# The experts' down product with the matmuls placed in column tiles of the array

## The reference, cut to what matters

```python
def expert_choice_ffn(x, w_router, w_gate, w_up, w_down):
    B, T, _ = x.shape
    cap = CAP_FACTOR * T // N_EXPERTS
    aff = jax.nn.softmax((x @ w_router).astype(jnp.float32), -1)
    gsel, idx = lax.top_k(jnp.swapaxes(aff, 1, 2), cap)
    bidx = jnp.arange(B)[:, None, None]
    xs = x[bidx, idx]
    hdn = jax.nn.silu(jnp.einsum('becd,edf->becf', xs, w_gate)) * jnp.einsum('becd,edf->becf', xs, w_up)
    out = jnp.einsum('becf,efd->becd', hdn, w_down) * gsel[..., None].astype(x.dtype)
    return jnp.zeros_like(x).at[bidx, idx].add(out)
```

## Time and profile before

| what | value |
|---|---|
| median of 3 runs | 3254.94 us (3253.11, 3254.94, 3256.28) |
| span of the profiled execution | 3254.3 us |
| PE busy | 3039.7 us, 93% |
| PE weight loads busy | 2229.6 us, 69% |
| DVE, ACT, POOL busy | 963.2, 577.3, 96.0 us |
| bytes over HBM | 517.89 MB read, 25.70 MB written |

### The profile page before, as it was taken

How to read it: one execution, slowest core, us unless ns; L and a number is a source line. 1 busy time by engine, 2 the same in 40 slices (tenths; PEclk the granted TensorE clock), 3 DMA queues, 4 the chain that set the end, 5 groups by cost and what they waited for, 6 DMA issues and landing times.

```text
span 3254.3 us, 43264 instructions
## 1 busy us (share of the span) xinstructions
PE 3039.7 (93%) x18405; PEld 2229.6 (69%) x18405; DVE 963.2 (30%) x2408; ACT 577.3 (18%) x1297; POOL 96.0 (3%) x145
## 2 busy tenths in 40 slices
PE   6999999797999999997999989999986999999994
PEld 1465479745887777771456459999944888777773
DVE  1100136643001000102177536666645010001002
ACT  3100111240000000003167212222242000000002
POOL 0000000000000000000000000000000000000000
PEclk9899998897999999998999999999997999999997
DMA  8411100217999999957411100000016899999992
GB/s 281 154 52 52 45 1 1 65 62 270 312 311 303 303 309 308 306 183 271 155 52 52 39 0 1 1 2 1 1 65 224 279 314 304 307 305 307 306 310 87
DMA packets 276365, 545.50 MB, mean 168 GB/s; under 512 B 15233, under 2 KB 23817, under 8 KB 276233
## 3 DMA queue, kind: packets, MB, share of 16 engines
q1 hardware_dynamic: 175049, 328.64, 29.4%
q10 hardware_dynamic: 93600, 188.75, 16.6%
q0 software_dynamic: 7584, 26.22, 3.2%
HBM read 517.89 MB, written 25.70 MB: 167 GB/s over the span
## 4 chain that ended last, share of the span: by engine, by line
PE 88%; DVE 6%; ACT 3%; DMA 2%; issue 1%; SPq 0%; DVEq 0%; POOL 0%; ACTq 0%
PE ps L1204 28%; PE ps L1215 14%; PE ps L803 8%; PE ps L813 6%; PE ps L760 5%; PE ps L1139 3%; PE ps L1101 3%; PE ps L804 2%; PE ps L1083 2%; PE ps L880 1%; PE ps L1115 1%; PE ps L791 1%; PE ps L950 1%; PE ps L966 1%; ACT L424 1%; ACT L423 1%
## 5 line engine op out<-in xcount | busy, mean ns | idle before, releaser
L1204 PEld LDWEIGHTS ps<-wk,slots 128*128 128x128 f32 x6144 | 691.1, 192 | 16.5 <-issue 16.0
L1204 PE MATMUL ps<-wk,slots 128*128 128x80 f32 x6144 | 689.9, 275 | 0.0
L1215 PE MATMUL ps<-qkv,og 128*80 128x512 f32 x1024 | 446.7, 594 | 2.4 <-DVE og L1748 1.3
L1215 PEld LDWEIGHTS ps<-qkv,og 128*80 128x80 f32 x1024 | 151.0, 150 | 275.5 <-issue 268.0
L803 PE MATMUL ps<-hT,slots 128*128 128x512 f32 x640 | 334.0, 604 | 3.1 <-ACT hT L455 3.1
L1204 PE MATMUL ps<-wk,qkv 128*128 128x80 f32 x2048 | 233.9, 275 | 0.0
L1204 PEld LDWEIGHTS ps<-wk,qkv 128*128 128x128 f32 x2048 | 231.3, 192 | 0.0
L804 PEld LDWEIGHTS ps<-hT,slots 128*128 128x128 f32 x640 | 123.5, 193 | 156.6 <-issue 156.6
L813 PE MATMUL ps<-slots,hT 128*128 128x512 f32 x480 | 209.3, 596 | 0.0
L760 PE MATMUL ps<-slots,cnd 128*2 128x512 f32 x384 | 172.0, 602 | 35.1 <-DVE x L1776 24.1
L1724 DVE COPY idc<-idT 80x1 uint32 (+1 forms) x32 | 4.8, 149 | 612.8 <-DMA moe_d<-og,idc 612.7
(11 more groups left out here) (261 smaller groups left out, 3228.5 us busy)
## 6 DMA issues: line engine op xcount, KB each, us to landing
slots<-in_w_gate_dram ACTq DMA_DIRECT2D x60, 2048.0 KB, 9.2
qkv<-in_w_down_dram SPq DMA_DIRECT2D x34, 2048.0 KB, 9.8
slots<-in_w_up_dram SPq DMA_DIRECT2D x32, 2048.0 KB, 10.2
qkv<-in_w_up_dram SPq DMA_DIRECT2D x32, 2048.0 KB, 7.8
qkv<-in_w_down_dram ACTq DMA_DIRECT2D x30, 2048.0 KB, 7.8
slots<-in_w_ada_dram SPq DMA_DIRECT2D x24, 2048.0 KB, 8.1
slots<-in_w_in_dram SPq DMA_DIRECT2D x16, 2048.0 KB, 8.1
slots<-in_w_out_dram SPq DMA_DIRECT2D x4, 2048.0 KB, 16.2
```

The source lines that it names most:

```text
L1204: ins = mm(PS[:, j, fb * CAP:(fb + 1) * CAP], slot[j][:, kt, fb * P:(fb + 1) * P], xsT[q][:, kt, :], start=(kt == 0), stop=(kt == KT - 1))
L1215: ins = mm(PS[0:CAP, 4 + j, :], hdT[:, ft, :], slot[4 + j][:, ft, :], start=(ft == 0), stop=(ft == KT - 1))
```

## The change

The 80 stationary columns of the down product are split. The 64 sample tokens go first: for each `ft` one matmul puts outputs 0 to 511 on partitions 0 to 63 of bank 4 and one puts outputs 512 to 1023 on partitions 64 to 127 of the same bank. An output on 64 partitions from 0 or 64 uses the left or the right half of the array's columns. Then the 16 prompt tokens: for each `ft` four matmuls with 256 outputs each, on partitions 0, 32, 64 and 96 (16 of each 32) of bank 5. Each matmul has its own weight load as before. ACT copies two pieces of 64 x 512 and four of 16 x 256 in place of two of 80 x 512; the first two wait for a new counter, `o_mm`, and the fetch of block 4 now stands behind them and waits for the end of the whole down product, as does block 5. DVE copies the token weights to the partitions where the outputs now stand: two copies of 64 and four of 16 in place of one of 80.

```diff
@@ POOL, scatter
-                    pool.wait_ge(S("o_ready"), L * PER["o_ready"] + e * 2 + 2)
+                    pool.wait_ge(S("o_ready"), L * PER["o_ready"] + e * 6 + 6)
@@ ACT, expert
+                    act.wait_ge(S("o_mm"), L * PER["o_mm"] + e + 1)
+                    if first is None:
+                        act.wait_ge(S("scattered"), L * PER["scattered"] + (e - 1) * 16)
                     for hf in range(2):
-                        act.wait_ge(S("moe_used"), L * PER["moe_used"] + e * 6 + (5 + hf))
-                        if hf == 0 and first is None:
-                            act.wait_ge(S("scattered"), L * PER["scattered"] + (e - 1) * 16)
-                        A(osb[q][0:CAP, hf * HC:(hf + 1) * HC], PS[0:CAP, 4 + hf, :], ACT.Copy,
-                          scale=gsc[q][0:CAP, :]).then_inc(S("o_ready"), 1)
-                        if hf == 0:
-                            load(4)
+                        A(osb[q][0:CAPS, hf * HC:(hf + 1) * HC], PS[64 * hf:64 * hf + 64, 4, :], ACT.Copy,
+                          scale=gsc[q][64 * hf:64 * hf + 64, :]).then_inc(S("o_ready"), 1)
+                    act.wait_ge(S("moe_used"), L * PER["moe_used"] + e * 6 + 6)
+                    load(4)
+                    for c in range(4):
+                        A(osb[q][CAPS:CAP, c * 256:(c + 1) * 256], PS[32 * c:32 * c + CAPP, 5, 0:256], ACT.Copy,
+                          scale=gsp[q][32 * c:32 * c + CAPP, :]).then_inc(S("o_ready"), 1)
@@ PE, down
                     for j in range(2):
                         pe.wait_ge(land[4 + j], e * 16 + (16 * moe_base(L, 4 + j) + 16))
-                        if not first:
-                            pe.wait_ge(S("o_ready"), L * PER["o_ready"] + e * 2 + (j - 1))
-                        for ft in range(KT):
-                            ins = mm(PS[0:CAP, 4 + j, :], hdT[:, ft, :], slot[4 + j][:, ft, :],
+                    if not first:
+                        pe.wait_ge(S("o_ready"), L * PER["o_ready"] + e * 6 - 4)
+                    for ft in range(KT):
+                        for j in range(2):
+                            ins = mm(PS[64 * j:64 * j + 64, 4, :], hdT[:, ft, 0:CAPS], slot[4 + j][:, ft, :],
                                      start=(ft == 0), stop=(ft == KT - 1))
-                        ins.then_inc(S("moe_used"), 1)
+                    ins.then_inc(S("o_mm"), 1)
+                    if not first:
+                        pe.wait_ge(S("o_ready"), L * PER["o_ready"] + e * 6)
+                    for ft in range(KT):
+                        for c in range(4):
+                            ins = mm(PS[32 * c:32 * c + CAPP, 5, 0:256], hdT[:, ft, CAPS:CAP],
+                                     slot[4 + c // 2][:, ft, (c % 2) * 256:(c % 2 + 1) * 256],
+                                     start=(ft == 0), stop=(ft == KT - 1))
+                    ins.then_inc(S("moe_used"), 2)
@@ DVE, pick
-                    V.tensor_copy(gsc[q][0:CAP, :], gsel[0:CAP, bass.ds(e, 1)]).then_inc(S("idx"), 1)
+                    for hf in range(2):
+                        V.tensor_copy(gsc[q][64 * hf:64 * hf + 64, :], gsel[0:CAPS, bass.ds(e, 1)])
+                    for c in range(4):
+                        ins = V.tensor_copy(gsp[q][32 * c:32 * c + CAPP, :], gsel[CAPS:CAP, bass.ds(e, 1)])
+                    ins.then_inc(S("idx"), 1)
```

More of the change, by code:

```diff
@@ L48 @@
 PER = dict(ada_ev=12, fin_r=5, fin_i=5, ab=1, ada_mm=12, afft=1, aff=1, fin_sq=5, fin_start=1, g1b=4, g1e=4, g2b=4,
-           gathered=256, gexp=32, gmm=1, h_chain=32, hidden=32, idx=16, logits=1, moe_used=96, o_ready=32,
+           gathered=256, gexp=32, gmm=1, h_chain=32, hidden=32, idx=16, logits=1, moe_used=96, o_ready=96, o_mm=16,
            omm=10, scattered=256, selt=1, sel=2, sme=1, sm=1, st_new=4, topk=1, x_moe=5, x_new=10, xs_a=64,
@@ L128, in backbone @@
         gsc = [sb(f"gsc{q}", [P, 1]) for q in range(2)]
+        gsp = [sb(f"gsp{q}", [P, 1]) for q in range(2)]
         xn_d = nc.dram_tensor("xn_d", [TOK, D], F32, kind="Internal").ap()
```

## The result

The changed kernel takes **3160.22 us** (median of 4 runs, 3159.49 to 3162.36), where the kernel before, run beside it, takes 3254.03 us. The ratio is 0.9711, 95% interval 0.9697 to 0.9724: 94 us less, where 3297 us was forecast. Rival 1, all tiles at once, is what happened, and a little better than it was priced.

What follows compares the result with a forecast made beforehand. PE was taken as the bound. Per expert 7.31 + 7.10 + 0.60 = 15.01 us against 13.80, +1.21 x 32 = +38.7 us, plus 3.7 us at layer ends, gave 3297 us; range 3150 to 3345.

Steps and rivals of the forecast that it cites:

- Rival 1: Down product: records for free tiles pass waiting ones, all tiles stream at once; 11.4 us per expert, 3181 us; chance 0.35.
- What bounds: Whole expert loop: PE's time is the kernel's time, 43.08 us per expert; a down-product microsecond counts 32 times.
- The order of starts: Down product: PE starts records only in program order, so just two stream at any time, whatever the number of tiles.
- a2: Down product: second record of the first tile's float32 matmul; letters name tiles, numbers the two records of a matmul.
- 33 units: Four-tile prompt part: 64 records, two at a time, each unit 0.215 us for streaming 256 columns; 7.10 us.
- two-tile part: Sample part of the down product: 32 records take 16 units and one more at the end, 17 x 0.43 = 7.31 us.
- Changes of division: Down product: three switches per expert, whole array to halves, to quarters, to whole; one at 0.1, two at 0.25, 0.6 us.
- The clock: PE during the narrow stationary matmuls: granted clock stays at 1.00 (2.4 GHz); costed at nothing.
- Copies: ACT and DVE around the down product: +1.24 and +0.6 us, exposed only at two layers' ends; +3.7 us.
- The cover: Expert loop: gather has 9.6 us of cover against 1.8, block fetches 28 us against 11; no PE wait.
- the forecast's own range: Whole kernel: 3275 without switching and end costs, to about 3340 with three switches of 0.59 us.
- rival 4: Down product: four-tile part three at a time, or Rival 1 eaten up by 1 us switches; 13.8 us, 3255 us; chance 0.04.

Runs made afterwards that it cites:

- the version in quarters: Changed kernel with each 64-column sample matmul split into two of 32 columns, so the whole down product is in quarters: 3156.09 us, ratio 0.9693.
- the run of the late fetch: Kernel before, with only the fetch of block 4 moved behind the second copy of the down product: 3254.81 us, ratio 0.9993.

## Why the prediction was wrong

- **What bounds** held: PE's pieces made the period, and a microsecond on the down product counted 32 times. So did the reading that spacing and not duration is the cost.
- **The order of starts** failed: "If PE starts records only in the order of the program, a2 must wait for a1, since they share a tile, and b1 must wait until a2 has started." In the profile after, b1 starts with a1 (1003.43 us), and c1 and d1 as well (1010.45 us). Each tile keeps its own order and holds up to four records. The rows of before could not show passing, since they have no two tiles side by side, and I took its absence for evidence. That put 33 units instead of 16 on the prompt part: 7.10 us against 3.58 measured. The 3.5 us x 32 = 113 us are nearly all of the 137 us between 3297 and 3160.
- The **two-tile part**: 7.31 us forecast, 7.09 measured; two at a time was right, the extra unit at the end was not, since the last two records run together. That is 7 us.
- **Rival 1's sizes**: it had 3.9 us for the prompt part from 64 starts 0.061 us apart, a distance that belongs to one tile. On four tiles records start much closer, and only the streaming is left: 16 x 0.216 = 3.45 us, as the version in quarters shows.
- **Changes of division**: 0.6 us forecast for three, besides the two parts. The one between the parts is 0.13 to 0.14 us and lies inside the 3.58; besides them stand only the 0.20 us by which the gate and up piece is longer behind quarters, and the 0.10 us of issue ahead of halves. 0.3 us less, 10 us in all. With the two terms above that accounts for 130 of the 137 us. Of the rest 5 us come from the base: the forecast subtracted 13.80 us, from start to start, where the piece of the chain with which the new pieces compare is 13.96 (0.16 x 32), and 1 us from the ends of the layers.
- **The clock** stayed at 1.00 in both layers' experts (776 to 1403 us and 2500 to 3100 us), as costed.
- **Copies**: 0.48 us for a piece of 16 x 256, 0.465 measured; the end of each layer +1.26 us (+1.24 forecast). The +0.6 us of DVE's copies before the first gather did not show: from the first copy to the first gate matmul the kernel before takes 775.50 - 765.47 = 10.0 us, and the changed one 773.77 - 763.97 = 9.8. Five useless matmuls that PE runs there hid it.
- **The cover** for gather, scatter and fetches held; the run of the late fetch shows it for the fetch alone.
- **The chances**: 0.35 stood on the case that came, and rival 1's range lay in the stated one down to 3150, so the time fell inside the range while its likeliest value was on the wrong side. Of the two pages of the Trainium skill that the prediction names, TensorE: Matmul & The Clock Gate ("What overlaps and what doesn't") has matmuls start strictly in program order. These runs disagree for records on different tiles: the prompt part took 3.58 us, where that order gives 7.10. The Trainium skill's rule that tiles operate independently (TensorEngine Tiling (Array Packing), Key Properties) is the one with which they agree, up to four records per tile.
- **Small slips** that decide nothing: the upper end of the forecast's own range comes to 3336, not 3340, and rival 4's 13.8 us with 3.7 us for the ends to 3259, not 3255.

## What to carry to other kernels

A product with few stationary columns can be put in column tiles and gets nearly the full factor, also in float32: 1.97 times on two tiles (13.96 against 7.09 us for 32 records of 512 columns) and 3.9 on four (13.92 against 3.58), if neighbours in the program go to different tiles or at most two float32 matmuls in a row go to one. Long runs on one tile lose the overlap without any warning, so the tile loop belongs inside the contraction loop. And where a trace has no instance of a mechanism, its silence is no evidence: price both sides, and let neither take the middle of the forecast.

## What the runs showed of the hardware

- A tile of the array holds up to four float32 matmul records (or two matmuls, which is the same here), one at work and three waiting, and records for other tiles pass the waiting ones. Runs of 2, 4, 8 and 16 records per quarter took 3.58, 3.61, 7.99 and 11.38 us.
- Four tiles stream four different moving operands of float32 at the same rate as one: every 0.216 us four records of 256 columns. With 512 columns, four tiles took 0.43 us too, but with two different operands.
- A change between halves and quarters costs 0.14 us.
- Where fetches never pause, this core draws 374 to 385 GB/s, and that bounds an expert at 35.3 us.
- After waits of at most 1.66 us per expert, three experts in a row, the granted clock fell to 0.50. It stayed there for 54.4 us, though PE was busy throughout with the gate and up products, and came back in the down product.
